# Attention, recurrence and tile norms put into one stage, and the table turns dealt out anew

## The reference, cut to what matters

```python
def hybrid_layer(x, ...):
    h = rms_norm(x, norm_mix_g)
    aq, ak, av, hq, hf, hi, hg, ga, gh = split_combined(h @ w_in)
    y_attn = sliding_window_attention(aq, ak, av, sinks)
    o = hgrn2_recurrence(silu(hq), hf, hi, lower_bound)      # per chunk:
    #   o_intra = tril(q_dec @ k_inv^T) @ v ; o_inter = q_dec @ state
    #   state   = decay * state + (k * exp(b_last - b))^T @ v
    o = rms_norm(o, hgrn_norm_g) * silu(hg)
    merged = sigmoid(ga) * (y_attn @ w_attn_proj) + sigmoid(gh) * (y_hgrn @ w_hgrn_proj)
    x = x + merged @ w_out
    x = x + peer_layer(rms_norm(x, norm_ffn_g), w_peer_q, peer_keys, peer_u, peer_v)
```

## Time and profile before

| what | value |
|---|---|
| median of 3 runs | 2431.93 us (2431.86 to 2433.99) |
| the profiled execution: its own time, and its span | 2441.25 us, 2439.4 us |
| busy share PE, DVE, ACT, POOL | 85%, 64%, 20%, 35% |
| PE clock granted, mean | 0.913 of full |
| DMA, mean over the span | 266 GB/s |
| load and store of one turn | 512 KB each |
| high part of a weight panel on ACT (L228), mean | 1058 ns |

### The profile page before, as it was taken

How to read it: one execution, slowest core, us unless ns; L and a number is a source line. 1 busy time by engine, 2 the same in 40 slices (tenths; PEclk the granted TensorE clock), 3 DMA queues, 4 the chain that set the end, 5 groups by cost and what they waited for, 6 DMA issues and landing times. The chain is left out here.

```text
span 2439.4 us, 24361 instructions
## 1 busy us (share of the span) xinstructions
PE 2082.1 (85%) x8036; PEld 1395.9 (57%) x8036; DVE 1564.6 (64%) x3433; ACT 484.1 (20%) x1053; POOL 844.0 (35%) x637
## 2 busy tenths in 40 slices
PE   5998869697978989999988989888766579989977
PEld 4765848565826976556555555555422257724445
DVE  4468654436999975666666666666777776346752
ACT  3344032112211320000000000000000221334541
POOL 3420024323300005666555455444676232300002
PEclk8998579898988999999999999999988789989999
DMA  7875849974564559999999999999999321100001
GB/s 274 323 280 192 311 157 364 344 272 164 205 234 163 210 213 401 402 402 402 402 403 403 404 402 402 402 402 402 402 400 402 152 92 61 52 22 1 1 35 69
DMA packets 203900, 648.09 MB, mean 266 GB/s; under 512 B 19840, under 2 KB 52736, under 8 KB 202496
## 3 DMA queue, kind: packets, MB, share of 16 engines
q1 hardware_dynamic: 118384, 335.60, 37.4%
q0 software_dynamic: 73728, 268.47, 27.9%
q10 hardware_dynamic: 11664, 42.47, 5.1%
HBM read 560.48 MB, written 85.98 MB: 265 GB/s over the span
## 5 line engine op out<-in xcount | busy, mean ns | idle before, releaser
L1527 PE MATMUL ps<-arena 128*128 128x512 f32 x1024 | 516.8, 652 | 143.2 <-DVE arena L1384 99.6
L1395 DVE CUSTOM_DVE_ANT_0 arena<-arena 128x1024 bf16<-128x1024 f32 x256 | 313.3, 1224 | 249.1 <-DMA arena<-u_rows,u_row 138.2
L1516 PE MATMUL ps<-rows_n,arena 128*128 128x256 f32 x2048 | 465.5, 380 | 0.0
L1516 PEld LDWEIGHTS ps<-rows_n,arena 128*128 128x128 f32 x2048 | 387.4, 190 | 95.7 <-issue 49.5
L1527 PEld LDWEIGHTS ps<-arena 128*128 128x128 f32 x1024 | 206.7, 208 | 398.9 <-issue 261.4
L1259 POOL DMA_INDIRECT arena<-u_rows,u_row x256 | 291.7, 1140 | 312.6 <-DMA gates<-arena 169.0
L1259 POOL DMA_INDIRECT arena<-in_v,expert x192 | 213.3, 1111 | 312.3 <-DVE arena L1416 283.3
L1416 DVE SCALAR_TENSOR_TENSOR arena<-arena,wt 128x1024 f32<-128x1024 f32 x192 | 246.2, 1282 | 0.4
L188 DVE STREAM_TRANSPOSE tdst<-tsrc 128x1024 f32<-128x1024 f32 x128 | 156.6, 1234 | 138.2 <-DMA u_rows<-tdst 137.7
L1493 ACT ACTIVATE ge<-dots 128x2 f32<-128x2 f32 x128 | 26.0, 203 | 906.3 <-DVE dots L1395 906.3
L232 POOL TENSOR_TENSOR in_wlo<-in_raw,in_whi 128x1024 fp32r<-128x1024 f32 x45 | 113.7, 2529 | 231.9 <-ACT in_whi L228 231.9
(11 more groups left out here) (388 smaller groups left out, 3002.2 us busy)
## 6 DMA issues: line engine op xcount, KB each, us to landing
tsrc<-in_u SPq DMA_DIRECT2D x128, 512.0 KB, 6.8
u_rows<-tdst SPq DMA_DIRECT2D x128, 512.0 KB, 4.7
arena<-in_u SPq DMA_DIRECT2D x128, 512.0 KB, 10.6
arena<-in_v SPq DMA_DIRECT2D x128, 512.0 KB, 11.8
in_raw<-in_panels ACTq DMA_DIRECT2D x37, 512.0 KB, 3.8
gates<-arena SPq DMA_DIRECT2D x8, 2048.0 KB, 8.8
arena<-gates SPq DMA_DIRECT2D x32, 512.0 KB, 18.8
mg_raw<-in_panels ACTq DMA_DIRECT2D x28, 512.0 KB, 6.6
```

The costliest lines, as they stand in the source:

```text
L1395: nc.vector.tensor_tensor_reduce(out=junk[:, n % 2], in0=u_slot[n % NU], in1=hrows[:, n // NPICK], scale=1.0, scalar=0.0, op0=ALU.mult, op ...
L1516: mm = nc.tensor.matmul(ps[:, j % 2, 0:TD], ud[:, j % RJ, k], rows_n2[:, 0, k], start=k == 0, stop=k == KD - 1)
L1527: mm = nc.tensor.matmul(ps[:, 4 + 2 * t + c], park[:, j % NPK, t * P:(t + 1) * P], vd[:, j % RJ, c * T:(c + 1) * T], start=j == 0, stop=j ...
```

## The change: what it does, and the diff

The stages wa and hg become one, called wh here, and it also takes the norm of the first three tiles out of hn. On every engine it is one loop over the 32 jobs. In iteration 2c stands chunk c, at iteration 8t+6 the output of tile t on PE, at 8t+7 the mean of its squares, at 8t+8 its seed on ACT and its norm on DVE. The scaling of the probabilities goes from DVE to ACT; the negated largest value is made in one DVE operation and not in two. The PSUM banks are divided: three for scores (four before), one each for turned probabilities, values, causal part, state and output. The recurrence has 4 state slots (8 before) and one masked buffer (two before). The exponential of the gate is freed after in1, and only its 64 last columns are kept (e_last). The stage hn keeps the last tile. The turns are now 38 in in1, 28 in wh, 38 in mg, 4 in n2, 20 in pq, and in mg their places are written out.

```diff
-TURNS = 30, 14, 20, 46, 2, 16
+TURNS = 38, 28, 38, 4, 20
...
-    eb = sb(b1c, "eb", [P, HG, T])
+    e_last = sb(b1c, "e_last", [P, HG, T // CHUNK])
...
-    bB = sb(b1b, "bB", [P, HG, T])
+    bB = kinv
+    eb = sb(b1b, "eb", [P, HG, T])
...
+        nc.vector.tensor_copy(e_last[:].rearrange("p h c -> p (h c)"), flat(eb)[:, :, CHUNK - 1])
...
-    specs += [own("exps", "act", both_exps, "b"),
+    specs += [own("exps", "act", both_exps, "b", "b last - b"),
...
+    def norm_tile(chain, t, mean):
+        s = slice(t * P, (t + 1) * P)
+        root(chain, kk[:, :, s], mean, kinv[:, :, s], kk[:, :, s])
+        chain(nc.vector.scalar_tensor_tensor(out=hf[:, :, s], in0=hf[:, :, s], scalar=vec("hgrn_norm_g"), in1=kk[:, :, s],
+                                             op0=ALU.mult, op1=ALU.mult))
+        return nc.vector.tensor_tensor(hg[:, :, s], hg[:, :, s], hf[:, :, s], ALU.mult)
...
-        attention_stage("wa", jobs, units, 2, T_WA, (sinks_loaded, 16))
...
+        n, NC_, NST = len(jobs), T // CHUNK, 4
+        SCORE, TURN, PV, AM, DS, OUT = (0, 1, 2), 3, 4, 5, 6, 7
+        chunk_at = {2 * c: c for c in range(NC_)}
+        tile_at = lambda i, x: (i - x) // 8 if i >= x and (i - x) % 8 == 0 and (i - x) // 8 < NT - 1 else None
...
+        for x in range(T_WH):
+            turn_in[1 + x * n // T_WH] += 1
...
+            def scores(i):
+                if i >= 3:
+                    pe.wait_ge(S["exp"], i - 2)
...
+            def turned(j):
+                pe.wait_ge(S["prob"], j + 1)
+                if j:
+                    pe.wait_ge(S["copied"], j)
...
+            def out(t):
+                pe.wait_ge(S["am"], t + 1)
+                if t:
+                    pe.wait_ge(S["y"], t)
+                pe.wait_ge(S["stt"], 4 * t + 3)
...
+            def mean(t):
+                pe.wait_ge(S["of"], t + 1)
+                pe.wait_ge(S["sq"], t + 1)
+                nc.tensor.matmul(by_head(OUT), cst("mean128"), kinv[:, :, cols(t)], start=True, stop=True).then_inc(S["mean"], 1)
...
+            keys_turned(0)
+            within(0)
+            for i in range(n + 4):
+                if i < n:
+                    scores(i)
+                if 3 <= i < n + 3:
+                    turned(i - 3)
+                if i - 4 in last_job:
+                    pv(last_job.index(i - 4))
+                if tile_at(i, 7) is not None:
+                    mean(tile_at(i, 7))
+                if i in chunk_at:
+                    c = chunk_at[i]
+                    if c < NC_ - 1:
+                        added(c)
+                    if c % 4 == 2 and c // 4 + 1 < NT:
+                        keys_turned(c // 4 + 1)
+                    if c % 4 == 3:
+                        if c // 4 + 1 < NT:
+                            within(c // 4 + 1)
+                        out(c // 4)
+
+        @block.vector
...
+            def next_state(c):
+                v.wait_ge(S["ds"], c + 1)
+                if c:
+                    v.wait_ge(S["stt"], c)
+                if c % 4 == 3:
+                    v.wait_ge(S["o"], c // 4 + 1)
...
+            for j in range(n + 4):
+                if j < n:
+                    largest(j)
+                if 1 <= j <= n:
+                    inverse(j - 1)
+                if j in chunk_at and chunk_at[j] % 4 == 0:
+                    masked(chunk_at[j] // 4)
+                for x in range(turn_in[j]):
+                    turner.turn(v)
+                if j - 4 in last_job and last_job.index(j - 4) % 2:
+                    unit_out(last_job.index(j - 4) // 2)
+                if j in chunk_at and chunk_at[j] < NC_ - 1:
+                    next_state(chunk_at[j])
+                if tile_at(j, 8) is not None:
+                    normed(tile_at(j, 8))
+                if tile_at(j, 10) is not None:
+                    low(tile_at(j, 10))
...
+            def scaled(j):
+                act.wait_ge(S["recip"], j + 1)
+                pr = prob[:, j % 4, 0:jobs[j]["n"]]
+                nc.scalar.activation(pr, pr, ACT.Copy, scale=rs[:, j % 4, 2:3]).then_inc(S["prob"], 1)
...
+            for j in range(n + 4):
+                if j < n:
+                    exps(j)
+                if 1 <= j <= n:
+                    scaled(j - 1)
+                if 3 <= j < n + 3:
+                    copied(j - 3)
+                if j in chunk_at and chunk_at[j] % 4 == 2 and chunk_at[j] // 4 + 1 < NT:
+                    keys_out(chunk_at[j] // 4 + 1)
+                if j % 8 == 7 and j // 8 < NT:
+                    tile_out(j // 8)
+                if tile_at(j, 8) is not None:
+                    act.wait_ge(S["mean"], tile_at(j, 8) + 1)
+                    seed_tile(tile_at(j, 8), ps[:, OUT]).then_inc(S["seed"], 1)
+                if tile_at(j, 9) is not None:
+                    act.wait_ge(S["y"], tile_at(j, 9) + 1)
+                    high_tile(tile_at(j, 9)).then_inc(S["hi"], 1)
...
+            nc.scalar.activation(kinv[:, :, t * P:], hf[:, :, t * P:], ACT.Square).then_inc(S["sq"], 1)
+            act.wait_ge(S["mean"], 1)
+            seed_tile(t, ps[:, 0]).then_inc(S["seed"], 1)
+            act.wait_ge(S["y"], 1)
+            high_tile(t).then_inc(S["hi"], 1)
             for i in range(2):
                 mg_weights.make_hi(act, i)
...
-        mms = list(range(5 * KD - 2))
-        panel_stage("mg", PAN["merge"], with_side(specs, lambda u, s: turns_after(u, mms, T_MG)), weights=mg_weights)
+
+        places = [4 * m for m in range(KD - 2) for x in range(4)] + [4 * KD - 4] * 2 + [4 * KD + m for m in range(KD - 2) for x in range(2)]
+        panel_stage("mg", PAN["merge"], with_side(specs, lambda u, s: sum(turns_after(x, range(len(places)), T_MG)
+                                                                          for x, y in enumerate(places) if y == u)),
```

More of the change, by code:

```diff
@@ L194, in program @@
     tdst = sbr(turn_st, "tdst", [P, 2, D])
-    T_IN, T_WA, T_HG, T_MG, T_N2, T_PQ = TURNS
-    assert T_IN + T_WA + T_HG + T_MG + T_N2 + T_PQ == EXP_N
+    T_IN, T_WH, T_MG, T_N2, T_PQ = TURNS
+    assert T_IN + T_WH + T_MG + T_N2 + T_PQ == EXP_N
     first_loads = ExitStack()
@@ new lines, in program @@
+        mx = sb(st, "wh_mx", [P, 4, 4])
+        rs = sb(st, "wh_rs", [P, 4, 4])
+        neg_sinks = sb(st, "wh_neg_sinks", [P, HEADS])
+        state = sb(st, "state", [P, NST, HG, P])
+        at = sb(st, "hgrn_a", [P, HG, P])
+        tok = kk
+        names = ("scores negmax exp sinkexp recip prob turned copied pv unit dve zero "
+                 "kturned tok a am ds stt o of sq mean seed y hi lo")
+        S = dict(zip(names.split(), sems(st, " ".join("wh_" + x for x in names.split()))))
@@ L934, in program @@
     with ExitStack() as st:
-        yt, rt, sq = kinv[:, 0:2], kinv[:, 2:4], kk
-        names = ("sq mean root r y hi lo dve").split()
+        t = NT - 1
+        names = ("sq mean seed y hi lo dve").split()
         S = dict(zip(names, sems(st, " ".join("hn_" + x for x in names))))
@@ L967, in _ @@
             pe.wait_ge(S["sq"], 1)
[L968 to L969 removed]
+            nc.tensor.matmul(ps[:, 0].rearrange("p (h s) -> p h s", h=HG), cst("mean128"), kinv[:, :, t * P:], start=True, stop=True
+                             ).then_inc(S["mean"], 1)
         @block.vector
         def _(v):
[L973 to L982 removed]
+            chain = Chain(v, S["dve"])
+            v.wait_ge(S["seed"], 1)
+            norm_tile(chain, t, ps[:, 0].rearrange("p (h s) -> p h s", h=HG)).then_inc(S["y"], 1)
+            v.wait_ge(S["hi"], 1)
+            low_tile(t).then_inc(S["lo"], 1)
     b1h.close()
```

261 lines of the change are left out of this document (141 added, 120 removed).

## The result

The changed kernel took 2471.24 us (median of 4 runs, 2468.33 to 2474.18), the kernel before, beside it, 2432.96 (2431.86 to 2438.74): a ratio of 1.0152, 95% interval 1.0132 to 1.0173, so 1.5% slower. The forecast was 2420.3, faster. The profiled execution took 2471.34 us.

The account below looks back on a forecast made before the run. Limits were taken to alternate by stage among DMA-fed turns, DVE and half-clocked PE. Terms -21 + 9 + 9.2 + 2.7 - 11.5 = -11.6 us, taken from the median 2431.93, gave 2420.3 us; range 2398 to 2440.

Parts of the forecast that it names:

- Joint stage: Merged wa and hg: 147 us for 144.3, +2.7, the middle between DVE-bound 128 and PE-bound 167.
- list of stalls: Three tile edges of the joint stage: output group, PE's mean, table loads; 7.3 to 15 us per edge.
- my two ends, 128 and 167: Joint stage: 128 us DVE-bound with PE at full clock, 167 us PE-bound at half clock.
- Rival B: Joint stage: output groups and pauses keep PE at 1.2 GHz; PE-bound at 167 us, total 2440; chance 0.13.
- in1: Input stage: eight more turns cost +9 us, bounds 0 and +23.
- less about 5 us of idle DMA time that gets used: in1: six more turns, 17.5 us, delay the last copy of values by only 12 to 13 us.
- PE's slack: in1: PE needs the last copy of values 5.3 us after its end, so it is 7 us late there.
- rival C: in1 finds no idle DMA time: +23 us and not +9, total 2434; chance 0.07.
- D: Theory of the follow-up experiments, not a forecast rival: turns cost DMA time where DMAs are full, as in in1.
- n2 and pq: More turns there: +4.5 us in n2 from waiting for stores, +4.7 in pq from DVE time, +9.2 together.
- Merge and w_out: mg: pause before the last m_lo shrinks from 24.0 to 2.6 us, w_out part +2 to +3; sum -21.
- Norm stage: hn with one tile left: about 14.5 us for 26.2, -11.5, bounds -15.3 and -8.

Follow-up runs that it names:

- Fill: Changed kernel with two score banks and three idle 512-column products per joint-stage job (108, output unread): 2444.46 us, ratio 1.0065.
- control: Changed kernel with two score banks, one turned bank and no idle products: 2466.58 us, ratio 1.0141.

## Why the prediction was wrong

The seven stages missed by +44.8 us together (from -11.6 to +33.2).

- **Joint stage, +27.1 for +2.7. This step failed**, above all in its list of stalls. DVE's sum was right (94 us, measured 94.3), and PE's too: 157 us at half clock and 92 at full give 141 at the measured 0.62 (an estimate, linear between the two), and 141.2 was measured. But PE stood still for 30 us of the stage. Of the one turned bank, which ACT empties behind norm and table loads, I had nothing; the second bank is worth 19.5 us at the same clock. The stall behind the output group I had named (2 to 8 us an edge) was there at 10 us each, but it was worth nothing by itself: without it DVE waited for the scores. The norm inside costs 15.7 us of stage for the 11.9 it saves.
- **The clock in it.** 0.62 lies inside the 0.6 to 0.75 that I had named, but the 147 us that I took belong to 0.75; my two ends, 128 and 167, give 158 at 0.62 (an estimate, in the same way). That is 11 of the 24 us missed. Fill against control shows that the clock counts: 21 us for 0.84 instead of 0.61. Rival B named a stage of 167 us, and it took 171.4. That was partly luck: B had 157 us of work and 10 of stalls, and there were 141 and 30.
- **in1, +21.8 for +9. This step failed too.** The step "less about 5 us of idle DMA time that gets used" was wrong, and with it PE's slack. Eight turns made the waits for stores 20.2 us longer, the DMA share rose only to 0.88, and the first values, not the last ones, stopped PE (16.3 us). I had seen that PE already waited for the first copy and that six more turns would stand before it, and then priced only the last. The usual size is 18.4 us, nearer to rival C's +23 than to +9. With the turns back in1 took 130.0, and the kernel before with these turns took 146.8 like the changed ones; so it was the turns, D, and not the moved exponentials.
- **n2 and pq, +13.3 for +9.2.** Right in kind: the third turn waited 4.6 us for its store; but the fourth waited too (1.3), and a turn in pq cost 1.6 us, later 1.8, not 1.2.
- **Merge and w_out, -16.9 for -21.** Right in kind: pause 5.0 us for 2.6, +1.8 behind it for 2 to 3. Of the 2.4 us more in the pause, 2.2 are the cast to m_hi, which fell beside an operation of POOL (last section). The 2 us of clock that I expected back did not come: the first 8 matmuls behind the pause took 3.56 us, 3.78 before. My reason, the number of turns ahead, was not the whole one: 31 do as well as 26.
- **Norm stage, -12.1 for -11.5.** Right.

The chances were at fault too. B and C had 0.13 and 0.07, as if one excluded the other; both came near, and the two sizes add.

On the table loads: the operation in front of the first ends at 270.98 and the load begins at 271.00; the seed ends at 272.98 and the second begins at 273.00. The Trainium skill, "ScalarE: Activation LUTs", What ACT_TABLE_LOAD costs, puts a drain of 1.38 us to each switch; the trace shows none in front of it and none behind.

## What to carry to other kernels

When two pipelines are put into one order, count the buffers between each pair of engines again: one bank emptied by an engine that now does something long in between can cost more (19.5 us here) than the operations saved are worth (10 us of DVE). The price of a background transfer depends on the stage and on its place there: a turn cost 2.3 us in in1, about 1 in the joint stage without the fill and 2.4 with it, and nothing for five more in the merge once they stood away from the merges. And compare by the part of the trace that was touched; the untouched rest moved by 14 us between executions, more than many of the effects.

## What the hardware showed

- A denser PE can be faster: 108 useless products made a stage 21 us shorter, since 0.22 us per product of 32 columns became 0.12. The same trick in hg cost 10 us, the clock going from 0.56 to 0.63 only. Three added products in the joint stage with 42 turns raised the clock too, for no gain; and 37 turns gave a shorter stage (150.7) than 34 (154.4). Both stay open; where in the jobs the turns fall was not varied.
- Some operations of DVE and of POOL make each other wait, and it is not always the same one that waits. The last m_hi took 2.61 us from 505.31 in the changed kernel; POOL had begun its operation at 505.30, for 2.34 us. Without POOL beside it the same cast took 0.43 us in the kernel before (at 490.05). One output tile earlier, again 0.01 us behind POOL's start, the cast took its 0.43; there POOL took 2.68, and m_lo waited and took 2.77 instead of 0.69. So it went in all seven tiles before the last (timeline of POOL, then of DVE):

```profile
488.98 2.68 POOL L232 TENSOR_TENSOR mg_wlo<-mg_raw,mg_whi 128x1024 fp32r<-128x1024 f32 x1 [3.05 <-ACT mg_whi L228]
...
505.30 2.34 POOL L232 TENSOR_TENSOR mg_wlo<-mg_raw,mg_whi 128x1024 fp32r<-128x1024 f32 x1 [3.04 <-ACT mg_whi L228]
```

```profile
488.99 0.43 DVE L1162 CAST m_hi<-part 128x512 fp32r<-128x512 f32 x1
489.45 2.77 DVE L1163 TENSOR_TENSOR m_lo<-part,m_hi 128x512 fp32r<-128x512 f32 x1
...
505.31 2.61 DVE L1162 CAST m_hi<-part 128x512 fp32r<-128x512 f32 x1
```

The Trainium skill, "Trainium Architecture — The Big Picture", What this means for kernel authors, says that DVE and GpSimd share a port pair as an exclusive lock. The trace agrees: the last cast ended 0.28 us after POOL's operation. It also shows that not every operation of DVE has to wait: a turn at 159.06, within POOL's operation of 157.70 to 160.08, took its usual 1.25 us.
